# Rearranging the two ends of an attention stage, and filling TensorE's last attention slots with unread products

## The chip, the cores and the metric

The kernel runs on one core of a Trainium2 chip. It is one program, launched once, and the metric is the device time of that launch in microseconds (us). Three runs of the kernel before took 1500.4, 1500.2 and 1497.41 us; their median is 1500.2. The engines are TensorE (PE in the profile, with its weight loads as PEld), VectorE (DVE), ScalarE (ACT), GpSimd (POOL), and SyncE (SP), which here issues every DMA.

## The reference

The reference is one layer of a streaming encoder for two groups of rows: 1024 prompt rows without a cache, and 64 decode rows with a cache of 256 keys. Cut to what matters here:

```
z = (rms_norm(x) * (1 + sc1) + sh1) @ w_in            # queries, keys, values, index queries
lam = exp(sum(lq1*lk1)) - exp(sum(lq2*lk2)) + 0.2
# 4 differential heads:
a = softmax(q1 k1 + bias) - lam * softmax(q2 k2 + bias)
o = rms_norm(a @ v) * g_subln * 0.8
# 8 sparse heads (2 key/value heads): keep the top-k keys of an indexer's score, then
o = softmax(q k + bias, kept keys only) @ v
m = concat(o_diff, o_sparse) @ w_out                  # 1024 x 1024
x = x + ga1 * rms_norm(m)
x = x + ga2 * rms_norm(swiglu(rms_norm(x) * (1 + sc2) + sh2))
```

Keys are visible by chunks of 64 positions, and the bias comes from a table of 32 buckets over key position minus query position. The new keys and values are outputs too.

## The kernel before, in words

Products that need float32 accuracy are made from two parts of each operand: a high part (the value rounded to TensorE's fp32r) and a low part (value minus high part). A product is then three matmuls: high by high, high by low, low by high.

The program has four stages, in the order of time: the input projection with its modulation and the top-k search (0 to about 372 us of the span), attention (372 to 670), the output projection (670 to 780), and the feed-forward network (to the end).

The input projection works through 21 blocks of 128 output columns (`BLOCKS`), each in three chunks of token columns (`chunk`). The last seven blocks but a few are query blocks. ACT copies each query block to `qst`, and SP stores it to `q_scratch` in HBM. Before the last block (`b == NB - 1`) SP loads heads 0 to 6 of the queries of token tile 0 into `qt`; head 7 of tile 0 and the whole of tile 1 are loaded after that block. ACT computes the two exponentials of lambda after the last block (line 1395), and DVE finishes lambda (line 1891).

Attention is a software pipeline written out by hand. There are nine token tiles `t` (eight of 128 prompt rows, one of 64 decode rows) and eight steps per tile (steps 0 to 3 are the differential heads, 4 to 7 the sparse ones, two heads a step), so `NSTEPS` = 72 steps. Each engine runs a loop over `SLOTS` = 78 slots. In a slot it works on different steps: PE makes the scores of step `s` = slot (`scores`), transposes the probabilities of step slot-3 (`transpose_probs`), makes the value products of step slot-4 (`value_products`), and transposes the normalised head of slot-6. DVE adds biases and finds row maxima of step `s` = slot (`biases`, line 1977), and scales the probabilities of slot-2 (`weights`, lines 1914 to 1991). ACT takes exponentials of slot-1 (line 1500) and copies transposed tiles out (`aT`, `oT`). Slots 72 to 77 have no new scores: they drain the pipeline. The order within each engine is the order of the code, and engines wait for each other by semaphores.

The biases come from HBM in expanded form. Tiles 0, 1 and 8 have theirs loaded in one go (`e_first`, `e_second`, `e_last`); tiles 2 to 7 use a ring of four (`ering`, `load_e`, line 909), two DMAs for each of 12 heads of a tile. The name `ering` stands in the trace for `e_second` too (line 927). SP issues all DMAs in the order of its code. After the ring's load number 8 of tile 2 it issues, in one go, the six loads of the decode rows' values (`load_decode_values`, lines 935 to 940), which are first read at slot 68.

While attention drains, the operands of the output projection are prepared. ACT rounds the weight rows to their high part (`oweh`, `split_out`, by the table `W_HIGH`), in the order `W_ORDER` = (4, 5, 6, 7, 3, 0, 1, 2), and the attention output of tile 0 (`oTh_first`, `high_out`). The low parts `owel` of weight blocks 4, 5, 6, 7 are subtracted on POOL in slots 68 to 71 (line 1180), those of 3, 0, 1, 2 on DVE in slots 73 and 74 (line 2042). DVE makes the low part of tile 0's attention output (`low_out(0)`, line 1907) in slot 72. `out_products` (line 2759) then makes, for each tile and each half of the columns, 8 blocks times 3 products; the first tile's first product waits for `o_lo` and the first `owel`. Tile 0 accumulates in the PSUM region called `S` in the trace, tile 1 in `PJ`.

## Time and profile before

| what | value |
|---|---|
| median of three runs | 1500.2 us |
| profiled execution, its time | 1499.62 us |
| its span (first to last instruction) | 1497.9 us |
| PE busy | 1421.3 us (95%) |
| DVE busy | 1065.1 us (71%) |
| ACT busy | 645.0 us (43%) |
| POOL busy | 323.0 us (22%) |
| mean granted TensorE clock | 0.974 |

The shares of busy time are averages over stages with different limits. The granted clock is 1.00 at TensorE's full speed of 2.4 GHz and 0.50 at 1.2 GHz. A row that ends in "[2.33 <-DVE ...]" says that the engine was idle for 2.33 us just before it, and what ended that.

### The profile page before, as it was taken

To read this page: it belongs to the slowest core of one execution; us is meant where nothing else is said; L and a number is where in the kernel's file an instruction comes from. 1 tells how busy PE (TensorE), PEld (TensorE's weight loads), DVE (VectorE), ACT (ScalarE), POOL (GpSimd) and SP (SyncE) were. 2 spreads that over 40 slices of the span, in tenths; PEclk is the share of its full clock that TensorE was granted. 3 is DMA by queue.
4 is the path that set the end of the run, shared out by engine and by line. 5 is a ranking of instruction groups with operands and counts; after the bars stand their busy time and mean duration, and the time that the engine had idled before them with its cause. 6 is when DMAs were issued, how large, how long until landed. Compare 5 with 4: busy or idle time off the path is not lost.

```text
span 1497.9 us, 26711 instructions
## 1 busy us (share of the span) xinstructions
PE 1421.3 (95%) x9519; PEld 1230.4 (82%) x9519; DVE 1065.1 (71%) x2317; ACT 645.0 (43%) x1362; POOL 323.0 (22%) x357
## 2 busy tenths in 40 slices
PE   5998999999789999989997999999999999999997
PEld 3775999899456666658887999999999999888876
DVE  4526999998789888783578666666566656875687
ACT  4546222222577776772564332233223332533353
POOL 3111111111111000030112543344334440000011
PEclk9999999999699999979999999999999999999999
DMA  9410456633555455532323323332333216995333
GB/s 298 126 50 17 133 178 202 204 111 99 113 157 153 145 137 136 117 113 78 115 83 100 97 89 114 86 104 80 114 114 111 73 58 227 307 322 190 115 89 141
DMA packets 180148, 198.28 MB, mean 132 GB/s; under 512 B 19757, under 2 KB 136814, under 8 KB 180058
## 3 DMA queue, kind: packets, MB, share of 16 engines
q1 hardware_dynamic: 180058, 197.11, 43.6%
q8 instruction: 52, 0.85, 0.2%
q14 instruction: 38, 0.31, 0.1%
HBM read 154.00 MB, written 43.08 MB: 132 GB/s over the span
## 4 chain that ended last, share of the span: by engine, by line
PE 86%; DVE 5%; ACT 3%; issue 2%; DMA 2%; SPq 1%; POOL 0%; DVEq 0%; POOLq 0%; ACTq 0%
PE PJ L2506 15%; PE S L2788 14%; PE S L2865 8%; PE T L2788 8%; PE PJ L2788 8%; PE S L2651 5%; PE PJ L2865 4%; PE T L2865 4%; PE S L2759 4%; PE T L2626 3%; PE PJ L2759 3%; PE PJ L2713 2%; PE PJ L2716 2%; PE S L2562 1%; PE S L2657 1%
## 5 line engine op out<-in xcount | busy, mean ns | idle before, releaser
L1794 DVE TENSOR_SCALAR_CACHE_REDUCE scrap<-work,cand 128x384 uint8<-128x384 f32 (+6 forms) x217 | 177.9, 884 | 1.1
L2506 PE MATMUL PJ<-hTh,wh 128*128 128x352 f32 (+2 forms) x480 | 160.7, 335 | 0.0
L2506 PE MATMUL PJ<-hTh,wl 128*128 128x352 f32 (+2 forms) x480 | 157.5, 328 | 0.0
L2506 PE MATMUL PJ<-hTl,wh 128*128 128x352 f32 (+2 forms) x480 | 157.4, 328 | 0.0
L662 POOL TENSOR_TENSOR wab_a<-graw,wab_a 128x512 fp32r<-128x512 f32 x63 | 87.4, 1401 | 247.0 <-ACT wab_a L1396 247.0
L1136 POOL TENSOR_TENSOR wl<-wraw,wh 128x1024 fp32r<-128x1024 f32 (+1 forms) x21 | 49.5, 2358 | 273.8 <-ACT wh L1230 273.8
L2098 DVE TENSOR_TENSOR mix_later<-mix_later,S 128x256 f32<-128x256 f32 (+1 forms) x147 | 60.9, 427 | 66.2 <-PE S L2788 65.2
L2788 PE MATMUL S<-tokA,wab_a 128*128 128x256 f32 x792 | 99.9, 285 | 0.2 <-ACT mix_later L1396 0.2
L2788 PEld LDWEIGHTS S<-tokA,wab_a 128*128 128x128 f32 x792 | 97.9, 193 | 0.6 <-issue 0.5
L2506 PEld LDWEIGHTS PJ<-hTh,wh 128*128 128x128 f32 (+1 forms) x480 | 90.6, 189 | 7.8 <-issue 6.4
L1396 ACT ACTIVATE aT<-T 128x512 f32<-128x512 f32 (+4 forms) x168 | 67.9, 452 | 56.2 <-PE T L2626 55.7
L2506 PEld LDWEIGHTS PJ<-hTl,wh 128*128 128x128 f32 (+1 forms) x480 | 90.8, 189 | 0.3
L2506 PEld LDWEIGHTS PJ<-hTh,wl 128*128 128x128 f32 (+1 forms) x480 | 90.4, 188 | 0.3
L2098 DVE TENSOR_TENSOR hid<-mix_later 128x256 f32<-128x256 f32 (+1 forms) x84 | 71.6, 852 | 25.8 <-ACT mix_later L1554 20.8
L1396 ACT ACTIVATE dhi<-draw 128x1088 fp32r<-128x1088 f32 (+2 forms) x77 | 64.1, 836 | 60.0 <-PE PJ L2865 22.7
L1977 DVE CUSTOM_DVE_ANT_0 sc<-S,ering 128x256 f32<-128x256 f32 (+6 forms) x84 | 65.9, 821 | 24.0 <-PE S L2651 12.9
L1500 ACT ACTIVATE sc<-sc,nmax 128x128 f32<-128x128 f32 (+8 forms) x108 | 79.7, 742 | 0.8 <-DVE nmax L1977 0.8
L1127 POOL TENSOR_SCALAR mss<-mss 128x1 f32<-128x1 f32 (+1 forms) x23 | 5.4, 237 | 303.1 <-ACT ysq L1681 197.0
L2865 PE MATMUL S<-dhi 128*128 128x512 f32 x176 | 68.6, 390 | 0.0
L2865 PE MATMUL S<-dlo,dhi 128*128 128x512 f32 x176 | 68.5, 389 | 0.0
L1549 ACT ACTIVATE mix_later<-mix_later 128x256 f32<-128x256 f32 (+1 forms) x42 | 18.1, 431 | 109.3 <-DVE mix_later L2098 109.3
L1554 ACT ACTIVATE mix_later<-mix_later 128x256 f32<-128x256 f32 (+1 forms) x42 | 17.8, 423 | 106.3 <-DVE mix_later L2098 106.3
(360 smaller groups left out, 3581.6 us busy)
## 6 DMA issues: line engine op xcount, KB each, us to landing
graw<-in_w_gu SPq DMA_DIRECT2D x44, 512.0 KB, 5.4
ada<-in_w_ada SPq DMA_DIRECT2D x16, 1024.0 KB, 7.3
draw<-in_w_down SPq DMA_DIRECT2D x55, 256.0 KB, 3.6
h_scratch<-hid SPq DMA_DIRECT2D x22, 544.0 KB, 3.5
s_scratch<-hsum SPq DMA_DIRECT2D x11, 1024.0 KB, 4.2
draw<-s_scratch SPq DMA_DIRECT2D x44, 256.0 KB, 3.7
wraw<-in_w_in SPq DMA_DIRECT2D x20, 512.0 KB, 5.8
draw<-h_scratch SPq DMA_DIRECT2D x33, 256.0 KB, 3.0
```

What stands on the lines that cost most here:

```text
L662: eng.tensor_tensor(weight_operand(q, 1), weight_source(s, q), weight_operand(q, 0).bitcast(F32), ALU.subtract).then_inc(g_lo, 1)
L1136: pool.tensor_tensor(wl[:, b % 2, :, 0:n], wraw[:, b % 2, :, 0:n], wh[:, b % 2, :, 0:n].bitcast(F32), ALU.subtract).then_inc(w_lo, 1)
L1396: act_copy = lambda out, in_, **kw: nc.scalar.activation(out, in_, ACT.Copy, **kw)
L1500: nc.scalar.activation(p, p, ACT.Exp, scale=-1.0, bias=nmax[0:r, s % 4, m:m + 1], accum_out=rsum[0:r, s % 4, m:m + 1]).then_inc(exp_done, 1)
L1794: ins = nc.vector.tensor_scalar(scrap[0:r, o:o + n], work[0:r, o:o + n], least_score, None, ALU.is_ge, ALU.add, accum_out=rows_at(count, i))
L1977: nc.vector.tensor_tensor_reduce(out=probs(s, m)[0:r, 0:n], in0=S[m][0:r, 0:n], in1=rev, scale=-1.0, scalar=3.0e38, op0=ALU.add, op1=ALU.m ...
L2098: nc.vector.tensor_tensor(to, a, b, op).then_inc(mixed, 1)
L2506: last = pe.matmul(chunk_bank(3 * b + c)[0:w, 0:n], wp[:, b % 2, k, 0:w], hp[:, k, c0:c0 + n], start=(k == 0 and p == 0), stop=(k == KB - ...
L2651: last = pe.matmul(S[m][0:r, o:o + w], qt[part, t % 2, i, 0:r], keys, start=True, stop=not kept)
L2759: last = pe.matmul(OUT[t % 2][0:r, cols_], op[:, k, 0:r], wp[:, k, cols_], start=(k == W_ORDER[0] and p == 0), stop=(k == W_ORDER[-1] and ...
L2788: last = pe.matmul(bank, weight_operand(q, wp)[:, k, :], token_operand(c, q, tp)[:, k, :], start=(k == 0 and p == 0), stop=(k == 3 and p = ...
L2865: last = pe.matmul(down_bank(s, j), ap, wp[:, 0:HD], start=(k == 0 and p == 0), stop=(k == HALF - 1 and p == len(parts) - 1))
```

## The change

Six things change. All are in or beside attention.

1. Heads 0 to 6 of the queries of tile 1 are loaded before the last projection block too (448 KB), right behind those of tile 0; head 7 of tile 1 (64 KB) follows behind head 7 of tile 0. The load of the whole tile 1 (512 KB), which stood behind the loads of `e_second`, is gone. PE waits for head 7 of tile 1 at step 15.
2. ACT makes lambda's exponentials, with the table load they need, between the first and the second chunk of the last projection block.
3. The six loads of the decode values are no longer issued together at tile 2, but one at a time behind ring loads 1, 2, 3, 7, 8 and 9 of tile 5.
4. POOL makes no low part of the output weights any more. All eight are made on DVE, four in slot 73 and four in slot 74.
5. `low_out(0)` moves on DVE from slot 72 to slot 73, and the first half of tile 0's output products is ordered by part: eight high by high products, then eight with the low part of the attention output, then eight with the low part of the weights, each with its own waits.
6. PE gets `IDLE_PRODUCTS` = 4 products at the end of each of slots 72 to 76, 20 in all: `identb` by `upto`, bf16 constants, 128x128 by 128x512, into a PSUM bank that nothing reads before it is overwritten. They wait for the last biases, since the bank held scores.

```diff
-W_LOW_POOL = {68: 4, 69: 5, 70: 6, 71: 7}
-W_LOW_DVE = {73: (3, 0), 74: (1, 2)}
+W_LOW = {73: (4, 5, 6, 7), 74: (3, 0, 1, 2)}
...
+IDLE_PRODUCTS = 4
...
                     load_q(0, 0, 7)
+                    load_q(1, 0, 7)
...
-                if t:
+                if t >= 2:
                     load_q(t, 0, 8)
...
             load_q(0, 7, 8)
+            sp.wait_ge(ld_q[1], 16)
+            load_q(1, 7, 8)
             load_tile(0)
...
-                if j == 8 and t == 2:
-                    load_decode_values()
+                if t == 5 and j in (1, 2, 3, 7, 8, 9):
+                    load_decode_values((1, 2, 3, 7, 8, 9).index(j))
...
-                if slot in W_LOW_POOL:
-                    k = W_LOW_POOL[slot]
-                    pool.wait_ge(ow_hi, W_ORDER.index(k) + 1)
-                    pool.tensor_tensor(owel[:, k, :], owraw[:, k, :], oweh[:, k, :].bitcast(F32), ALU.subtract
-                                       ).then_inc(ow_lo_p, 1)
...
+                    if b == NB - 1 and c == 0:
+                        act.wait_ge(lam_ready, 1)
+                        nc.scalar.activation(lam[:, 2:4], lam[:, 0:2], ACT.Exp).then_inc(lam_ready, 1)
...
-                if slot == NSTEPS:
+                if slot == NSTEPS + 1:
                     low_out(0)
-                for k in W_LOW_DVE.get(slot, ()):
+                for k in W_LOW.get(slot, ()):
...
                 if i == 0:
-                    pe.wait_ge(ld_q[t % 2], 16 * (t // 2 + 1))
+                    pe.wait_ge(ld_q[t % 2], 16 * (t // 2 + 1 + (t % 2 if t > 1 else 0)))
+                if t == 1 and i == 7:
+                    pe.wait_ge(ld_q[1], 32)
...
+                if NSTEPS <= slot < SLOTS - 1:
+
+                    pe.wait_ge(biased, 2 * NSTEPS)
+                    for _ in range(IDLE_PRODUCTS):
+                        pe.matmul(S[1][:, 512:1024], identb[:, :], upto[:, 0:512], start=True, stop=True)
...
+                first = t == 0 and half == 0
+                order = [(p, k) for p in (0, 2, 1) for k in ks] if first else [(p, k) for k in ks for p in range(3)]
```

On SP, between the projection's last blocks and attention, the order before is this (`qt` is filled with queries, `vsbp` with values, `ering` at line 927 is `e_second`):

```order
L886 DMA q_scratch<-qst 128x1088 [waits chunk_out] x2
L864 DMA qt<-q_scratch 128x7x128 [waits q_stored1,q_stored0,score_acc]
L886 DMA q_scratch<-qst 128x1088 [waits chunk_out]
L864 DMA qt<-q_scratch 128x128 [waits r_stored,score_acc,q_stored1,ada_used,nat_stored1,chunk_done,q_stored0,nat_stored0]
L920 DMA vsbp<-out_dv_p 128x512
L921 DMA vsbp<-out_sv_p 128x128
L927 DMA ering<-r_scratch 64x12x192
L927 DMA ering<-r_scratch 64x12x256
L864 DMA qt<-q_scratch 128x8x128
```

The same place on SP in the changed kernel:

```order
L887 DMA q_scratch<-qst 128x1088 [waits chunk_out] x2
L864 DMA qt<-q_scratch 128x7x128 [waits q_stored1,q_stored0,score_acc]
L864 DMA qt<-q_scratch 128x7x128
L887 DMA q_scratch<-qst 128x1088 [waits chunk_out]
L864 DMA qt<-q_scratch 128x128 [waits r_stored,score_acc,q_stored1,ada_used,nat_stored1,chunk_done,q_stored0,nat_stored0]
L864 DMA qt<-q_scratch 128x128 [waits ld_q1]
L921 DMA vsbp<-out_dv_p 128x512
L922 DMA vsbp<-out_sv_p 128x128
L930 DMA ering<-r_scratch 64x12x192
L930 DMA ering<-r_scratch 64x12x256
```

The big load of tile 1's queries has moved from behind `e_second` to a place ahead of the last query store, and one 64 KB load stands newly ahead of the values and of `e_second`.

On DVE at the end of attention (slots 72 to 74 and the first work behind them), before:

```order
L1914 RECIPROCAL rinv<-rsum 64x2 [waits exp_done]
L1988 TENSOR_SCALAR sc<-sc,rinv 64x320 [waits vchain]
L1988 TENSOR_SCALAR sc<-sc,rinv 64x320
L2016 TENSOR_SCALAR ob<-ob,oss 64x128 [waits o_rms]
L1907 TENSOR_TENSOR oTl_116<-oT_94,oTh_first 128x1024 [waits o_hi]
L1914 RECIPROCAL rinv<-rsum 64x2 [waits exp_done]
L1988 TENSOR_SCALAR sc_last<-sc_last,rinv 64x320 [waits vchain]
L1988 TENSOR_SCALAR sc_last<-sc_last,rinv 64x320
L2042 TENSOR_TENSOR owel<-owraw,oweh 128x1024 [waits ow_hi] x4
L1907 TENSOR_TENSOR oTl_117<-oT_95,oTh 128x1024 [waits o_hi]
```

The same place on DVE in the changed kernel:

```order
L1914 RECIPROCAL rinv<-rsum 64x2 [waits exp_done]
L1988 TENSOR_SCALAR sc<-sc,rinv 64x320 [waits vchain]
L1988 TENSOR_SCALAR sc<-sc,rinv 64x320
L2016 TENSOR_SCALAR ob<-ob,oss 64x128 [waits o_rms]
L1914 RECIPROCAL rinv<-rsum 64x2 [waits exp_done]
L1988 TENSOR_SCALAR sc_last<-sc_last,rinv 64x320 [waits vchain]
L1988 TENSOR_SCALAR sc_last<-sc_last,rinv 64x320
L1907 TENSOR_TENSOR oTl_116<-oT_94,oTh_first 128x1024 [waits o_hi]
L2042 TENSOR_TENSOR owel<-owraw,oweh 128x1024 [waits ow_hi] x8
L1907 TENSOR_TENSOR oTl_117<-oT_95,oTh 128x1024 [waits o_hi]
```

The low part of tile 0's output now stands behind the last probabilities, and eight weight subtractions follow it instead of four.

On PE from the last value products (slots 74 and 75) to the first output products, before:

```order
L2713 MATMUL PJ<-aT_92,vsbd 64x64 [waits pair_read,t_freed1,t_freed0]
L2713 MATMUL PJ<-aT_92,vsbd 64x64 x5
L2713 MATMUL PJ<-aT_112,vsbd 64x64 [waits pair_read,t_freed0,t_freed1]
L2713 MATMUL PJ<-aT_112,vsbd 64x64 x5
L2759 MATMUL S<-oweh,oTh_first 128x512 [waits ow_lo_p,o_lo]
L2759 MATMUL S<-owel,oTh_first 128x512
L2759 MATMUL S<-oweh,oTl_116 128x512
L2759 MATMUL S<-oweh,oTh_first 128x512 [waits ow_lo_p]
```

The same place on PE in the changed kernel:

```order
L2715 MATMUL PJ<-aT_92,vsbd 64x64 [waits pair_read,t_freed1,t_freed0]
L2715 MATMUL PJ<-aT_92,vsbd 64x64 x5
L2752 MATMUL S<-upto,identb 128x512 [waits biased]
L2752 MATMUL S<-upto,identb 128x512 x3
L2715 MATMUL PJ<-aT_112,vsbd 64x64 [waits pair_read,t_freed0,t_freed1]
L2715 MATMUL PJ<-aT_112,vsbd 64x64 x5
L2752 MATMUL S<-upto,identb 128x512 [waits biased]
L2752 MATMUL S<-upto,identb 128x512 x3
L2752 MATMUL S<-upto,identb 128x512 [waits biased]
L2752 MATMUL S<-upto,identb 128x512 x3
L2775 MATMUL S<-oweh,oTh_first 128x512 [waits ow_hi,o_hi] x8
L2775 MATMUL S<-oweh,oTl_116 128x512 [waits o_lo] x8
```

Eight unread products stand between the last value product and the first output product, and the output products no longer ask for a low part of the weights before their seventeenth.

## Rows read from the trace of the kernel before

**Rows 1.** Busy time by stretch: attention's start.

```profile
372.00:403.00 31.00, 23.75 (x104) 13.77 (x104) 18.64 (x104) 18.53 (x73) 5.61 (x12) 0.56 0.63 142
```

Columns of such a row: stretch and its length in us; busy us (and count) of PE, PEld, DVE, ACT, POOL; granted clock; DMA share; GB/s.

**Rows 2.** Timeline at attention's start, of ACT, POOL and DVE (start, duration).

```profile
372.63 1.28 ACT L1395 ACT_TABLE_LOAD   x1
...
372.15 0.73 POOL L1155 MEMSET e_first<- 64x768 f32 x1 [19.82 <-PE PJ L2506]
...
374.38 0.29 DVE L1977 CUSTOM_DVE_ANT_0 sc<-S,e_first 128x128 f32<-128x128 f32 x1
```

**Rows 3.** Loads of `e_second`: timeline of SP, and size with us to landing.

```profile
376.83 1.29 SPq L927 DMA_DIRECT2D ering<-r_scratch  x2
...
ering<-r_scratch SPq DMA_DIRECT2D x1, 768.0 KB, 10.4
```

**Rows 4.** Timeline of PE: the scores of steps 8 and 9.

```profile
389.45 1.23 PE L2651 MATMUL S<-kTp,qt 64*128 64x256 f32 x4 [3.36 <-DMA qt<-q_scratch]
...
392.25 1.23 PE L2651 MATMUL S<-kTp,qt 64*128 64x256 f32 x4
```

**Rows 5.** The decode values' loads: SP and DVE, and a stretch behind.

```profile
423.17 0.59 SPq L935 DMA_DIRECT2D vsbd<-in_c_dv  x1
...
430.27 0.56 DVE L1977 CUSTOM_DVE_ANT_0 sc<-S,ering 128x384 f32<-128x384 f32 x1 [2.98 <-DMA ering<-r_scratch]
...
430.30:437.00 6.70, 6.11 (x25) 4.42 (x27) 6.25 (x23) 1.66 (x4) 1.15 (x2) 0.50 0.45 121
```

**Rows 6.** The ring's loads in tile 5: timeline of SP, issue to landing.

```profile
503.38 34.73 SPq L909 DMA_DIRECT2D ering<-r_scratch  x24
...
DMA to landing us min/median/max: 3.0/3.4/4.4
```

**Rows 7.** Attention's end, POOL and DVE: timeline, and one group of lines by form.

```profile
662.04 2.34 POOL L1180 TENSOR_TENSOR owel<-owraw,oweh 128x1024 fp32r<-128x1024 f32 x1
...
648.56 2.30 DVE L1916 SCALAR_TENSOR_TENSOR rlam<-rinv,lam,rsum 64x1 f32<-64x1 f32 x1
...
661.28 3.28 DVE L1988 TENSOR_SCALAR sc<-sc,rinv 64x320 f32<-64x320 f32 x2
...
L1988 DVE TENSOR_SCALAR sc<-sc,rinv 64x320 f32<-64x320 f32 x6 | 8.8, 1502 | 0.1
...
666.00 0.68 DVE L1988 TENSOR_SCALAR sc_last<-sc_last,rinv 64x320 f32<-64x320 f32 x2
666.59 4.61 DVE L2042 TENSOR_TENSOR owel<-owraw,oweh 128x1024 fp32r<-128x1024 f32 x4
```

**Rows 8.** Timeline of ACT in slots 69 to 72.

```profile
650.15 1.06 ACT L1396 ACTIVATE oweh<-owraw 128x1024 fp32r<-128x1024 f32 x1
...
658.77 0.55 ACT L1500 ACTIVATE sc<-sc,nmax 64x320 f32<-64x320 f32 x1
...
659.87 1.04 ACT L1396 ACTIVATE oTh_first<-oT 128x1024 fp32r<-128x1024 f32 x1
660.82 0.65 ACT L1396 ACTIVATE aT<-T 128x128 f32<-128x128 f32 x4
```

**Rows 9.** Stretches around idle times of PE, in attention and in the next stage.

```profile
649.50:651.50 2.00, 0.21 (x3) 0.01 (x1) 1.97 (x3) 1.71 (x5) 1.35 (x1) 1.00 0.10 39
652.50:670.00 17.50, 13.00 (x87) 8.01 (x86) 17.29 (x33) 13.06 (x41) 8.93 (x8) 0.50 0.01 2
...
801.50:804.00 2.50, 0.14 (x2) 0.14 (x2) 2.50 (x5) 2.03 (x4) 0.00 (x0) 1.00 0.00 0
804.00:808.00 4.00, 4.00 (x32) 4.00 (x32) 3.97 (x6) 0.00 (x0) 2.88 (x1) 1.00 0.00 0
```

**Rows 10.** PE: bf16 products of the same size, and timeline at attention's end.

```profile
L2657 PE MATMUL S<-keep,identn 128*128 128x512 bf16 x16 | 4.1, 382 | 0.0
...
669.40 1.10 PE L2713 MATMUL PJ<-aT,vsbd 128*64 128x64 f32 x12 [0.80 <-ACT aT L1396]
...
684.03 0.39 PE L2759 MATMUL PJ<-oweh,oTh 128*128 128x512 f32 x1
```

More of the change, by code:

```diff
@@ L864, in load_q @@
                 sp.dma_start(qt[:, t % 2, i0:i1, 0:r], q_dram[i0:i1, :, 128 * t:128 * t + r]
-                             .rearrange("b p t -> p b t")).then_inc(ld_q[t % 2] if i0 == 0 else ld_q7, 16)
+                             .rearrange("b p t -> p b t")).then_inc(ld_q7 if t == 0 and i0 else ld_q[t % 2], 16)
             for b in range(NB):
@@ L1392, in _ @@
                     row_out(j)
-            act.wait_ge(lam_ready, 1)
-            nc.scalar.activation(lam[:, 2:4], lam[:, 0:2], ACT.Exp).then_inc(lam_ready, 1)
             act_copy = lambda out, in_, **kw: nc.scalar.activation(out, in_, ACT.Copy, **kw)
```

51 lines of the change are left out of this document (29 added, 22 removed).

## The prediction, made before the changed kernel was run

> **What bounds the kernel now.** I read the split by stretch first, with the granted clock, then the list of who waited for whom inside attention, then the timeline of each engine at three places, then the sizes and landing times of DMAs there. PE is busy 95% of the span, so a change that leaves PE's own work alone can only win where PE stands or runs at its low clock. Attention holds three such places. At its start the granted clock is 0.56 on average and PE is busy 23.75 of 31 us [rows 1]. There PE stands 3.36 us for the queries of tile 1 [rows 4]. At 427 us DVE stands 2.98 us for a ring load that SP issued behind the six loads of the decode values, and the clock is 0.50 for the 6.7 us after it [rows 5]. From 652.5 to 670 us the clock is again 0.50, PE is busy 13.00 of 17.5 us and DVE 17.29 [rows 9]: DVE is the bound there, with work that takes much longer than it should [rows 7]. Outside these places I let everything move as one block, because between them the waits go from engine to engine and no transfer has a fixed date.
>
> **The start.** Lambda first. Before, DVE's first bias runs at 374.38, behind ACT's table load of 1.28 us that ends at 373.91 [rows 2]. With the exponentials inside the last block nothing holds that bias but PE's scores and the corner that POOL clears, ready at 372.15 + 0.73 = 372.9 [rows 2]. So slots 0 to 7 can begin up to 1.5 us sooner. That does not pass to the end, since slot 8 meets another limit, below. ACT's table load is hidden by its idle time between chunks; if it were not, it would cost its 1.28 us once.
>
> The queries: the scores of step 8 no longer wait. What is late next is `e_second`, the biases of step 8. Its second DMA is issued at about 376.83 + 0.65 = 377.5 and lands 10.4 us later, at 387.9 [rows 3]. One 64 KB load, some 0.4 us of SP, now stands ahead of it: 388.3. The 448 KB load is long over by then. From there the two bias operations of step 8, of 256 columns, take less than twice the 0.56 us of the 384-column form [rows 5]; I take 0.85. The scores of step 9 then start at about 389.15, where they started at 392.25 [rows 4]. They gain 3.1 us, because the transposes and value products of slot 8 (2.80 - 1.23 = 1.6 us of PE) now lie inside the wait for `e_second` instead of behind it. Bounds: if `e_second` lands 1 us later because other loads have moved ahead, 2.1; if it lands 1 us sooner with no 512 KB behind it, 4.1. From slot 9 on PE is busy without a gap before and after.
>
> The Trainium skill, "DMA: Bandwidth & Descriptors", section "Queues, rings and completion order", says that completion does not follow the order of issue on one engine. By that, `e_second` shared its time with the 512 KB issued behind it, which was down by 389.4 [rows 4], only 1.5 us after it. By the order of issue the landing stays at 388.3; by sharing it would come earlier, near the 4.1 end. No run here shows which yet.
>
> **The decode values.** The DVE wait of 2.98 us [rows 5] goes: the six loads took SP from 423.17 on, each about 0.6 us with the gap to the next, 3.2 us together, so the ring load behind them lands some 3.2 us earlier and is just in time. PE does not stand there, so the low clock of 430.3 to 437 goes too. It was worth little: DVE was busy 6.25 of those 6.70 us [rows 5], so at most 0.45 us was lost; I take 0.5 with the start of the next slot. Sum 3.5 us, between 3.0 and 4.0. In tile 5 each of the six loads adds 0.6 us to SP between ring loads. There 24 ring DMAs, two for each load, are spread over 34.73 us and land in 3.4 us [rows 6], so one ring load comes every 2.9 us and holds SP for 1.2 of it. The ring is four loads deep, 11.6 us on the average; I count nothing.
>
> **The end.** POOL's four subtractions cost 2.34 us each and lie on DVE's work. The clearest pair: POOL works from 662.04 to 664.38, and DVE's two scalings take 3.28 us from 661.28; the same two, with POOL idle, take 0.68 [rows 7]. Six of them took 8.8 us instead of 6 x 0.34 = 2.0, and a 64x1 operation took 2.30 us for what I take as 0.2. That is 8.9 us of stretched DVE time that goes. Against it DVE gets four more subtractions at 4.61 / 4 = 1.15 us [rows 7].
>
> With DVE free the next bound is ACT. Its chain from the end of the third `oweh` copy, 650.15 + 0.95 = 651.1 (such copies follow each other in 0.95 us, 659.87 to 660.82 [rows 8]), to the last transposed probabilities: six copies of 128x1024 (5.7 us), three pairs of exponentials at 1.10 (658.77 to 659.87; 3.3), three and a half groups of four transpose copies at 0.65 (2.25), and six small copies at 0.2 (1.2). Sum 12.45, so it reaches 663.55, and step 71's copies end at 664.2. The last value products start at 664.3, where they started at 669.40 [rows 10].
>
> Then the unread products. The first twelve lie in waits that PE has anyway. The last eight stand on the path: eight times 0.227 us at full clock. That price is from the output products (512 columns at 2.4 GHz are 0.213 us, and their rows at full clock step by 0.227), of which 48 follow each other from 669.40 + 1.10 = 670.5 to 684.03 [rows 10], part of them at the low clock; at 0.227 each 48 take 10.9 us, so 2.6 us were lost to the clock. The bf16 products of the same size in the trace keep PE 4.1 / 16 = 0.26 us each [rows 10], the other bound. So value products 0.6, eight unread 1.8: the output products start at 666.7. DVE's last low part comes at: exponentials of step 71 done at 658.7, scalings to 659.6, then nine subtractions at 1.15, 669.95. The seventeenth product, the first that reads a low weight, starts at 666.7 + 16 x 0.227 = 670.3, so none waits. At full clock the 48 end at 677.6 against 684.03: 6.4 us, less 0.4 for hand-overs that a chain without gaps leaves out, 6.0.
>
> Sum: 3.1 + 3.5 + 6.0 = 12.6 us, from the profiled execution's 1499.6 to 1487.0. The median of the runs is 0.6 above that execution, so 1487.6; I say 1487.5.
>
> **The rivals.** A, the forecast: the clock stays high through the drain. For it: PE's idle times shrink to about 1.4 us each, and unread products lie between. Chance 0.40.
>
> B: the clock falls there all the same. In the trace it fell after PE had stood 1.8 of 2.0 us, and it stayed at 1.00 after PE had stood 2.36 of 2.5 us [rows 9]. So an idle time alone does not decide. My replay leaves two idle times, about 659.7 to 661.2 and 662.6 to 664.3, with 1.5 us of work between, so it is open. Price: value products 1.1, eight unread ones at 0.427 = 3.4, start 668.8; the clock comes back 6.8 us after 664.3 as it did after 669.40 (670.5 + 2.6 / 0.2 = 13 products at 0.427, to 676), so five output products at the low clock and 43 at 0.227: 680.9, 3.3 us worse. Time 1490.8, chance 0.33.
>
> The Trainium skill, "TensorE: Matmul & The Clock Gate", Part 1, says that the point where the clock changes differs from run to run of one kernel. By it A and B would both occur among the runs, and the median would lie anywhere between 1487.5 and 1490.8. It is why I hold neither far above the other.
>
> C: the clock also stays high at the start, since PE's first wait, for the biases that began at 374.38 [rows 2], ends some 1.4 us sooner. Slots 8 to 12 ran at 0.50 with PE as the bound, 2.80 us a slot [rows 4]; at full clock four of them save about 0.7 us each. Time 1484.7, chance 0.12.
>
> D: the start's gain goes to `e_second` or another late transfer and only 0 to 1 us is left of 3.1. Against it: 10.4 us of landing already includes the traffic of that time. Time 1490.1, chance 0.10.
>
> E, slower: each decode load now makes its own stall. Before, six together cost 2.98 us and a fall of the clock. If in tile 5 each of them held the next ring load past its date, six waits would come. The price passes the whole gain of 12.6 us when each wait exceeds 2.1 us; at 3 us each, 18 less 12.6 gives 1505. It decides only if the ring's slack is used up. A load has to be issued and down in the time in which the two or three ahead of it are used, at least 2 x 2.9 = 5.8 us; it needs 1.2 + 0.6 + 3.4 = 5.2. That is closer than the average, but the wait would be tenths, not microseconds. Chance 0.03. The last 0.02 are for no change, if the stretched DVE work came from something else and the ends cancelled.
>
> **How the numbers follow.** A's own range is 1485.5 to 1489.5, from the bounds of the start (1 us either way), the middle (0.5) and the price of the unread products. With B, C and D taken in, 8 in 10 lie in 1483 to 1492.5. Faster by more than 0.2% (3 us), about what a measurement of this kernel can tell from no change, needs less than 1497.2: A to D, 0.95. Within: 0.02. Slower: 0.03.
>
> **What would show it.** In the changed profile: no wait of PE for `qt` at step 8 but one of DVE for `ering` near 388; no gap near 427 and none in tile 5; the scalings of steps 68 to 70 at 0.68 us a pair; ACT without gaps from slot 69 to 74; the output products of tile 0 taking 10.9 us, not 13.5. It is wrong if the pairs stay long with POOL idle, if products seventeen on wait for `owel`, or if the stages behind attention do not simply start earlier.

## The result: 10 us faster, and three attention segments that each tell their share

The changed kernel took 1490.19 us (median of five runs, 1488.58 to 1492.15), the kernel before 1500.2 in the runs beside them (1497.41 to 1502.34). The ratio is 0.9938 with a 95% interval of 0.9925 to 0.995, so it is faster by 0.5 to 0.75%. The forecast was 1487.5, with a range of 1483 to 1492.5. A second set of runs of the same kernel gave 1490.98, ratio 0.9935 (0.9918 to 0.9951).

The profiled execution took 1492.15 us, the longest of the five, with a span of 1490.4. I read it against the profile before between five marks on PE: the scores of step 0, of step 9 and of step 68, the first output product of tile 0, and the first of tile 1. Each column of the table below is the time in us from one mark to the next. Where nothing between two marks differs, such times often agree to tenths of a microsecond, while the totals of single runs differ by 3 to 5 us. The table holds every kernel of the study; the labels are explained with the experiments.

| kernel | scores 0 at | to scores 9 | to scores 68 | to output tile 0 | to output tile 1 | to the last product |
|---|---|---|---|---|---|---|
| before | 372.12 | 20.13 | 251.93 | 26.25 | 13.60 | 805.77 |
| changed | 376.80 | 15.48 | 245.31 | 26.43 | 11.09 | 807.25 |
| before_again | 373.83 | 19.05 | 252.05 | 26.26 | 13.64 | 805.76 |
| after_again | 375.40 | 15.08 | 247.60 | 26.34 | 11.12 | 806.63 |
| lambda_back | 375.00 | 14.77 | 249.14 | 26.46 | 11.11 | 807.01 |
| queries_back | 373.41 | 18.16 | 248.36 | 26.51 | 11.11 | 806.62 |
| decode_back | 373.45 | 15.08 | 251.82 | 25.90 | 11.11 | 806.60 |
| pool_low | 374.04 | 15.03 | 248.34 | 30.50 | 11.09 | 805.58 |
| no_unread | 374.33 | 15.07 | 247.79 | 21.45 | 13.10 | 805.59 |
| by_block | 374.16 | 15.14 | 247.50 | 21.47 | 12.94 | 805.59 |
| unread_early | 373.98 | 14.95 | 248.74 | 21.60 | 12.83 | 806.68 |
| search_gated | 374.68 | 16.75 | 245.45 | 21.48 | 13.38 | 806.65 |
| act_relieved | 373.18 | 17.06 | 248.01 | 18.05 | 13.39 | 805.57 |
| relieved_unread | 371.57 | 16.68 | 248.27 | 18.75 | 12.64 | 805.64 |

In the first pair of profiles attention came 4.68 us later, was 13.60 us shorter (311.91 to 298.31), and the stages behind it took 1.48 us more: 7.4 us in all. In the second pair attention went from 311.00 to 300.14, 10.86 us: 3.97 at the start, 4.45 in the middle, 2.44 at the end. Two pairs do not separate what the change gives from what differs from run to run. The experiments do, one edit at a time: 3.1 us at the start, 3.6 in the middle, 2.3 to 2.4 at the end, 9.1 in all.

**The start.** The first row is the stretch of [rows 1] in the changed kernel, the others two later stretches of it (columns as there):

```profile
372.00:403.00 31.00, 24.50 (x139) 15.54 (x137) 25.81 (x136) 18.70 (x78) 6.74 (x16) 0.83 0.59 131
...
380.00:390.00 10.00, 9.46 (x41) 6.25 (x42) 8.99 (x55) 6.15 (x28) 2.35 (x7) 0.51 1.01 205
390.00:400.00 10.00, 8.39 (x56) 4.48 (x57) 7.96 (x38) 8.30 (x34) 0.63 (x2) 0.98 0.60 123
```

The clock is 0.83 on the mean, against 0.56. It is low only from 380.2 to 390.4. PE's timeline where [rows 4] were:

```profile
388.75 1.23 PE L2653 MATMUL S<-kTp,qt 64*128 64x256 f32 x4
...
392.28 0.70 PE L2653 MATMUL S<-kTp,qt 64*128 64x256 f32 x4 [1.07 <-DVE nmax L1977]
```

The 3.36 us for `qt` are gone. What PE waits for now is DVE's step 8, and DVE stood before it:

```profile
391.45 0.42 DVE L1977 CUSTOM_DVE_ANT_0 sc<-S,ering 128x256 f32<-128x256 f32 x1 [1.65 <-issue]
```

SP's timeline has the two loads of `e_second`, and the row of DMA issues has the size of the second with its us to landing:

```profile
380.04 1.28 SPq L930 DMA_DIRECT2D ering<-r_scratch  x2
...
ering<-r_scratch SPq DMA_DIRECT2D x1, 768.0 KB, 10.7
```

It was issued at 380.04 + 0.63 = 380.7 and landed at 391.3. The profile names no releaser for DVE's 1.65 us, but they end 0.1 us behind this landing. That is the load that the prediction named as next late.

**The drain.** PE's timeline from slot 72 on, to be read against [rows 10]; L2752 are the unread products:

```profile
650.58 0.34 PE L2741 MATMUL T<-ident,ob 64*128 64x64 f32 x1 [1.30 <-ACT aT L1396]
650.85 1.89 PE L2752 MATMUL S<-upto,identb 128*128 128x512 bf16 x4
652.67 0.90 PE L2626 MATMUL T<-ident,sc 64*128 64x64 f32 x6
653.50 1.10 PE L2715 MATMUL PJ<-aT,vsbd 128*64 128x64 f32 x12
...
654.93 1.89 PE L2752 MATMUL S<-upto,identb 128*128 128x512 bf16 x4
...
658.62 1.89 PE L2752 MATMUL S<-upto,identb 128*128 128x512 bf16 x4
660.44 1.11 PE L2715 MATMUL PJ<-aT,vsbd 128*64 128x64 f32 x12
661.48 2.89 PE L2752 MATMUL S<-upto,identb 128*128 128x512 bf16 x8
664.02 2.19 PE L2775 MATMUL S<-oweh,oTh_first 128*128 128x512 f32 x8
```

From 650.58 on no row has an idle time: PE is the bound, and it works at half speed. Four unread products step by 1.82 us (650.85 to 652.67), twice the price that the prediction took. The clock by stretch:

```profile
646.00:650.00 4.00, 2.71 (x28) 1.70 (x25) 3.06 (x14) 3.84 (x13) 1.45 (x4) 0.98 0.02 4
650.00:656.00 6.00, 5.36 (x27) 2.69 (x28) 3.90 (x8) 5.71 (x20) 0.00 (x0) 0.50 0.01 3
656.00:660.00 4.00, 4.00 (x24) 1.90 (x22) 4.00 (x5) 2.16 (x7) 0.00 (x0) 0.50 0.00 0
660.00:664.00 4.00, 4.00 (x22) 1.75 (x21) 4.00 (x5) 1.23 (x2) 0.00 (x0) 0.56 0.32 83
```

It fell at 649.9, before the first unread product, and was back at 663.5. DVE has what the prediction said, where [rows 7] had 3.28 us for a pair:

```profile
649.45 0.67 DVE L1988 TENSOR_SCALAR sc<-sc,rinv 64x320 f32<-64x320 f32 x2
...
654.31 9.15 DVE L2042 TENSOR_TENSOR owel<-owraw,oweh 128x1024 fp32r<-128x1024 f32 x8
```

### The profile page after: what moved, and what is told of

Its sections match the earlier page's. It is cut to its first block, busy times and chain, and to the rows that moved or that the text cites. A ratio compares the mean times of both kernels' runs of the same rounds, so it can differ in the third digit from the quotient of the medians.

```text
span 1490.4 us, 26760 instructions
## 1 busy us (share of the span) xinstructions
PE 1421.1 (95%) x9539; PEld 1228.7 (82%) x9539; DVE 1067.2 (72%) x2321; ACT 644.5 (43%) x1362; POOL 313.8 (21%) x353
## 4 chain that ended last, share of the span: by engine, by line
PE 71%; DVE 21%; ACT 3%; issue 3%; DMA 1%; SPq 0%; POOL 0%; DVEq 0%; POOLq 0%; ACTq 0%
PE S L2805 15%; DVE scrap L1794 13%; PE PJ L2805 8%; PE T L2805 7%; PE S L2882 7%; PE S L2653 5%; PE T L2882 4%; PE S L2775 4%; PE PJ L2506 3%; PE PJ L2882 3%; PE T L2626 3%; PE PJ L2775 3%; PE PJ L2715 2%; PE PJ L2718 2%; PE S L2562 1%
```

## The experiments

Three groups shared their runs of the kernel before: no_unread, pool_low, queries_back and decode_back; after_again, before_again, unread_early and search_gated; lambda_back, by_block and act_relieved. relieved_unread has its own. Each ratio is to the runs of before in its own group.

### no_unread: the changed kernel without the unread products

```diff
-IDLE_PRODUCTS = 4
+IDLE_PRODUCTS = 0
```

> The changed kernel without the 20 unread products; nothing else differs. In its profile the clock had fallen to 0.50 at 649.9, before the first unread product (650.85); twelve of them stood on PE's path at 1.82 us per four, and PE was busy without a gap from 650.58. Theory 1 (they are a cost): ACT's chain becomes the bound (aT of step 71 ready near 657.9), the output products of tile 0 start 4.5 to 5 us earlier (near 659 against 664.02), they run some 11 to 14 of 48 at the low clock (0.427 instead of 0.227 us each, 2.2 to 2.8 us), and tile 1's first product comes 2 to 2.8 us earlier than 675.1. Total 1.5 to 3 us less than the changed kernel. Theory 2 (they bring the clock back, which is worth what they cost): without them PE has gaps until 659 and the low clock lasts into the output products for 30 of 48 or more; total 0 to 2 us more than the changed kernel.

Measured: 1487.1 us, ratio to before 0.9931 (0.9915 to 0.9946). PE in its drain:

```profile
650.17 0.34 PE L2741 MATMUL T<-ident,ob 64*128 64x64 f32 x1 [1.29 <-ACT aT L1396]
...
654.25 0.33 PE L2741 MATMUL T<-ident,ob 64*128 64x64 f32 x1 [1.66 <-ACT aT L1396]
...
657.61 1.10 PE L2715 MATMUL PJ<-aT,vsbd 128*64 128x64 f32 x12 [0.95 <-ACT oT L1396]
658.64 3.78 PE L2775 MATMUL S<-oweh,oTh_first 128*128 128x512 f32 x8
662.22 2.43 PE L2775 MATMUL S<-oweh,oTl 128*128 128x512 f32 x8
```

The waits are ACT's again, the output products start at 658.64, and the first eight take 3.58 us at the low clock:

```profile
660.00:664.00 4.00, 4.00 (x12) 3.10 (x11) 4.00 (x4) 0.00 (x0) 0.00 (x0) 0.61 0.94 359
```

From scores 68 to output tile 1 it takes 34.55 us instead of 37.46 to 37.52. Theory 1 holds, 0.1 us beyond the 2 to 2.8 us that it gave: the unread products cost 2.9 us net. The clock fell at 649.5 here and came back at 663.1, and with them at 649.9 and 663.5. It was low for 13.65 us in both, and back 25.9 us behind scores 68 in both, so they did not bring it back sooner: they put the output products off by 5.0 us (26.43 against 21.45), into a time of full clock, where these take 2.0 us less (11.09 against 13.10). The medians differ by 3 to 4 us, but against their own runs of before the two kernels differ by only 0.6 to 1 us (0.9931 against 0.9938 and 0.9935), with intervals that overlap. So the claim rests on the traces.

### pool_low: four low parts back on POOL

```diff
-W_LOW = {73: (4, 5, 6, 7), 74: (3, 0, 1, 2)}
+W_LOW_POOL = {68: 4, 69: 5, 70: 6, 71: 7}
+W_LOW = {73: (3, 0), 74: (1, 2)}
```

> The changed kernel, with the low parts of weight blocks 4, 5, 6, 7 back on POOL in slots 68 to 71 (order by part and unread products stay). Theory 1 (POOL's subtraction stretches DVE's operations while it runs): the pairs of scalings of steps 68 to 70 take about 2.9 us again instead of 0.67, DVE is the bound of the drain, from the scores of step 68 to the value products of step 71 it takes 25 us or more instead of 22.9, and the total is 2 to 4 us above the changed kernel. Theory 2 (the stretch had another cause, such as the low clock or the traffic of the loads): the pairs stay at 0.67 and the total is within 0.5 us of the changed kernel.

Measured: 1494.78 us, ratio 0.9972 (0.9961 to 0.9982). DVE and POOL in slot 70:

```profile
650.87 2.75 DVE L1995 TENSOR_SCALAR sc<-sc,rinv 64x320 f32<-64x320 f32 x2
```

```profile
650.81 2.34 POOL L1186 TENSOR_TENSOR owel<-owraw,oweh 128x1024 fp32r<-128x1024 f32 x1
```

The three pairs take 2.77, 2.75 and 3.28 us, each beside a POOL subtraction, and a 64x1 operation takes 2.31. From scores 68 to output tile 1 it is 41.59 us, 4.1 more than the changed kernel. Theory 1 holds; its 2 to 4 us were a little low. It is also 1.7 us more than before (39.85): with the stretch in place and the unread products added, the drain is longer than it was.

### queries_back: tile 1's queries loaded behind `e_second`

```diff
-                    load_q(1, 0, 7)
...
-                if t >= 2:
+                if t:
                     load_q(t, 0, 8)
...
-            sp.wait_ge(ld_q[1], 16)
-            load_q(1, 7, 8)
```

> The changed kernel, with tile 1's queries loaded behind the second bias load again. PE stands 3 us or more at step 8. Theory 1 (as I predicted, only the wait itself): 3 us more than the changed kernel, and the slots behind it run at the same clock as with the queries early. Theory 2 (the wait also keeps the clock low until about slot 12): the clock comes back near 400 instead of 390, slots 9 to 12 take 2.4 to 2.8 us instead of 1.6, and the total is 5 to 7 us above the changed kernel. Theory 3 (the early return of the clock was chance): the clock comes back near 390 to 394 all the same, 2 to 3 us more.

Measured: 1494.04 us, ratio 0.9968 (0.9956 to 0.9979). PE at step 8:

```profile
388.77 1.23 PE L2648 MATMUL S<-kTp,qt 64*128 64x256 f32 x4 [3.18 <-DMA qt<-q_scratch]
```

The wait is back. Scores 0 to 9 take 18.16 us instead of the 15.08 of after_again: 3.1 us. From scores 9 to 68 it is 248.36, between the 247.5 and 249.1 of its neighbours. The clock came back 11.6 us behind scores 9 (at 403.2), against 10.5 to 11.2 in after_again, decode_back, pool_low and no_unread. So theory 1 holds, and theory 2 (that the wait keeps the clock low) falls.

### decode_back: the six loads together at tile 2

```diff
-                if t == 5 and j in (1, 2, 3, 7, 8, 9):
-                    load_decode_values((1, 2, 3, 7, 8, 9).index(j))
+                if j == 8 and t == 2:
+                    for n in range(6):
+                        load_decode_values(n)
```

> The changed kernel, with the six loads of the decode values issued together at tile 2, load 8. Theory 1 (SP's queue): DVE stands about 3 us for the ring's load behind them (where the profile before had it at 427), PE's clock falls there, and the total is 3 to 4 us above the changed kernel. Theory 2: with attention's start earlier the ring is not ahead any more or less than before, and the wait is hidden by PE: 0 to 1 us.

Measured: 1493.22 us, ratio 0.9966 (0.9954 to 0.9979). DVE:

```profile
426.59 0.56 DVE L1978 CUSTOM_DVE_ANT_0 sc<-S,ering 128x384 f32<-128x384 f32 x1 [3.13 <-DMA ering<-r_scratch]
```

The wait of [rows 5] is back, and scores 9 to 68 take 251.82 us. The nine variants with spread loads whose clock behaved alike there have 247.50 to 249.14, mean 248.2. The difference is 3.6 us, and theory 1 holds. A rest of the wait is left near 425 us in six of the eleven profiles with spread loads, 0.2 to 0.65 us; the two with the longest (lambda_back and unread_early) have the two longest middles.

By ratio the totals of pool_low, queries_back and decode_back lie 4.2 to 5.5 us above the changed kernel, 0.6 to 1.9 us more than their times between marks. Their intervals are wide enough for both.

### after_again and before_again: each kernel once more

No edit. They ask which differences of the first pair of profiles belong to the change.

> The changed kernel once more. In its first profile the clock at attention's start fell at 380.6 and was back at 390.6, and from the scores of step 9 to those of step 68 it took 245.3 us; the three variants that keep the loads of the decode values spread took 247.8 to 248.4 there, with the low clock from about 377 to 401. Theory 1 (the early return was chance): this time 247.5 to 248.5 us, clock low until 398 to 403, and the attention from the first scores to the first product of the second output tile takes 300.5 to 301.5 us instead of 298.3. Theory 2 (it belongs to this kernel): 245 to 246 us again.

> The kernel before once more, for its profile. In its first profile three of DVE's small operations in the top-k search ran into a POOL subtraction (4.8 us in excess of 0.17 us each) and the search ended at 369.5, ahead of PE; in all five profiles of changed kernels there were five such (8.6 to 10.9 us), the search ended at 373.0 to 376.4 and PE waited 1.6 to 1.8 us. Theory 1 (it differs from run to run): five collisions and a search that ends at 372 or later can come here too, with a first score some 1.5 to 2 us later than 372.1. Theory 2 (the change causes it): three collisions and 369.5 again. From the first scores on both expect 311 to 312.5 us to the first product of output tile 1.

Measured, after_again: 1490.98 us, ratio 0.9935 (0.9918 to 0.9951); scores 9 to 68 in 247.60 us and 300.14 in all. The clock stayed low until 401:

```profile
390.00:400.00 10.00, 10.00 (x42) 4.90 (x41) 5.78 (x27) 6.92 (x28) 0.00 (x0) 0.50 0.33 86
```

Theory 1 holds: the early return in the first profile differs from run to run, and is worth 2 to 3 us. Of the eleven other profiles of changed kernels search_gated had it too; in act_relieved the clock came back at 388.3 and was low again from 391.7 to 401.9.

Measured, before_again: 1500.37 us in its one run. PE waits for the top-k search before the first scores, as in every changed kernel without the gate:

```profile
373.62 0.28 PE L2614 MATMUL T<-ident,gates 128*32 128x128 f32 x1 [1.77 <-DVE lam L1886]
```

Five small operations of the search ran into POOL's subtractions (0.78 + 1.71 + 2.38 + 2.28 + 2.35 = 9.5 us for what takes 0.85), and the search ended at 373.6 instead of 369.6. Theory 1 holds: a late search needs no change of the kernel, though how often the kernel before has one, two profiles can't say. The profile of before on which the prediction rests was one in which the search ended early.

### lambda_back: the exponentials behind the last projection block

```diff
-                    if b == NB - 1 and c == 0:
-                        act.wait_ge(lam_ready, 1)
-                        nc.scalar.activation(lam[:, 2:4], lam[:, 0:2], ACT.Exp).then_inc(lam_ready, 1)
...
+            act.wait_ge(lam_ready, 1)
+            nc.scalar.activation(lam[:, 2:4], lam[:, 0:2], ACT.Exp).then_inc(lam_ready, 1)
```

> The changed kernel with lambda's exponentials behind the last projection block again. Theory 1 (as I predicted: what lambda gives is taken back at step 8, where the bias load is late next): the first bias is 1.5 us or more later behind the first scores (2.2 instead of 0.62), but from the first scores to those of step 9 it takes at most 0.5 us more than 15.1. Theory 2 (the profiles of the variants show no wait for that load; PE at its low clock is the bound of slots 4 to 8, so lambda's 1.6 to 2.0 us are kept): 16.7 to 17.1 us from the first scores to those of step 9, and the attention from the first scores to tile 1's first output product 1.6 to 2.0 us longer than 300.1.

Measured: 1491.54 us, ratio 0.9938 (0.9917 to 0.996). Neither theory: the first bias stands 0.62 us behind the first scores (375.62 and 375.00), as with the edit, and scores 9 come after 14.77 us. PE and DVE wait for the search here, and ACT's table load is over by then. before_again, without the edit, has 0.62 us there too (374.45 and 373.83). In this state of the search the lambda edit gives nothing. In the first profile of before, with the search early, it would have given up to the 1.64 us by which that first bias was later (2.26 against 0.62).

### by_block: output products ordered by weight block again, on no_unread

```diff
-order = [(p, k) for p in (0, 2, 1) for k in ks] if first ...
+order = [(p, k) for k in ks for p in ((0, 2, 1) if first else range(3))] if first ...
```

> The kernel without unread products, with the first half of tile 0's output products ordered by weight block again (for each block high by high, low by high, high by low). Theory 1 (the order by part is what lets them start before the low weights are there): DVE has finished the first low part about 3 us before they start and needs 1.15 us for each further one, three products at the low clock need 1.28 us and at full clock 0.68; from the time the clock is back they would catch up with DVE near the sixth block and wait 0 to 1 us in all. Theory 2 (the order does nothing once DVE starts early): from the last value products to tile 1's first product 14.1 us as in the kernel without unread products, within 0.3. Both expect a small number; a wait for owel in the trace decides.

Measured: one run, 1486.6 us. PE has no wait for `owel`, and from the scores of step 68 to output tile 1 it takes 34.41 us against 34.55. Theory 2: with DVE free early, the order by part gives nothing that one profile could tell.

### unread_early: the unread products in slots 70 to 73

```diff
-                if NSTEPS <= slot < SLOTS - 1:
-                    pe.wait_ge(biased, 2 * NSTEPS)
+                if 70 <= slot < 74:
+                    pe.wait_ge(biased, 2 * min(slot + 1, NSTEPS) - 2)
```

> The changed kernel with the unread products in slots 70 to 73, four each, instead of 72 to 76. They now begin at about 647, while the clock is still high (it fell at 649.3 to 649.9). Theory 1 (PE's idle times make the clock fall, and products in them prevent it): the clock stays at 1.00 through the drain; the value products of step 71 come at ACT's pace, about 20.4 us behind the scores of step 68 as without unread products, tile 0's 48 output products take 10.9 us, and from the scores of step 68 to tile 1's first product it takes 32 to 33 us (37.5 in the changed kernel, 34.6 without unread products). Theory 2 (the clock falls all the same, since PE has too little dense work for longer than this): 36 to 37.5 us, because eight to twelve of them run at 0.43 to 0.47 us each on the path.

Measured: 1488.48 us, ratio 0.9923 (0.9906 to 0.9939). The clock was still high where it had been low in both other versions:

```profile
650.00:656.00 6.00, 3.53 (x39) 2.05 (x34) 3.99 (x9) 5.89 (x20) 0.02 (x1) 1.00 0.01 3
656.00:660.00 4.00, 3.95 (x34) 2.91 (x33) 4.00 (x4) 2.97 (x9) 0.00 (x0) 0.54 0.00 0
```

It fell at 656.3, in spite of them. The segment takes 34.43 us, as without any. So neither theory's number: products put where the clock is high do hold it for a while, and here the gain and the price were equal.

### search_gated: POOL's subtractions in the projection kept off the search's small operations, on no_unread

```diff
+SEARCH_GATE = {11: 157, 12: 179, 13: 212, 14: 234, 15: 267,
+               16: 289, 17: 311, 18: 344, 19: 355, 20: 377}
...
             for b in range(2, NB):
+                if b in SEARCH_GATE:
+                    pool.wait_ge(vchain, SEARCH_GATE[b])
                 low_w(b)
```

> The kernel without unread products, in which POOL's subtraction of the low part of each projection weight block from 11 to 20 waits until the first count of a chosen round of the top-k search is over, so that it lies beside DVE's long counting operations and not beside the four small ones between rounds. Theory 1 (a small DVE operation stands for as long as POOL's subtraction runs, the long ones do not): no small operation of the search over 0.3 us behind 215 us of the span, the search ends at 363 to 366 instead of 373 to 374, PE does not wait for lambda's copy, the first scores come 1.5 to 1.9 us earlier, at 372 to 372.5; total 1.5 to 2 us below the kernel without unread products if nothing else gives. Theory 2 (the long operations are stretched as well): the search ends within 2 us of 373. Theory 3 (the gates hold the low weights back too long): PE stands for them, and the total is slower by what it stands.

Measured: 1487.32 us, ratio 0.9917 (0.9902 to 0.9932). The pairs behind this experiment, POOL and DVE in the changed kernel:

```profile
282.89 2.38 POOL L1140 TENSOR_TENSOR wl<-wraw,wh 128x1024 fp32r<-128x1024 f32 x1 [13.55 <-ACT wh L1229]
...
282.97 2.33 DVE L1843 TENSOR_SCALAR step<-step 128x7 f32<-128x7 f32 x1
```

A 128x7 operation took 2.33 us because POOL had begun 0.08 us earlier. The same operation by form between 215 and 365 us, in the changed kernel and in the gated one (busy us, mean ns):

```profile
L1843 DVE TENSOR_SCALAR step<-step 128x7 f32<-128x7 f32 x21 | 7.9, 378 | 0.7
```

```profile
L1846 DVE TENSOR_SCALAR step<-step 128x7 f32<-128x7 f32 x22 | 3.8, 170 | 0.7
```

All four kinds of small operation have 166 to 170 ns now, the long counting ones their old times, and the search ends at 365.4 instead of 373 to 376. So theory 1 holds for the search. It does not for the total: PE did not wait for the search, yet its first scores came at 374.68, because its own clock had been 0.83 in the stretch from 140 to 160 us, as in the first profile of the changed kernel. The gain against no_unread cannot be told from nothing. Where the first scores did come early, loads took most of it back: in relieved_unread, gated too, they came at 371.57, but scores 9 only 16.68 us later, where the profiles with early queries and without the gate have 14.8 to 15.5. PE stood 1.31 us there for a load of values (`vsbp`) and 0.31 us behind `e_second`.

### act_relieved: ACT's copies of the drain moved, on search_gated

```diff
-W_HIGH = {67: (4,), 68: (5,), 69: (6,), 70: (7,), 72: (3, 0), 73: (1, 2)}
+W_HIGH = {66: (4,), 67: (5,), 68: (6,), 69: (7,), 72: (3,), 73: (0,), 74: (1, 2)}
...
-                if slot == NSTEPS - 1:
+                if slot == NSTEPS - 7:
                     high_out(0)
```

> The kernel without unread products and with the gated search, with ACT's eight copies of the drain moved: the high part of tile 0's output in slot 65 instead of 71, the high parts of weight blocks 4, 5, 6, 7 in slots 66 to 69 instead of 67 to 70, those of 3, 0, 1, 2 in slots 72, 73, 74, 74 instead of 72, 72, 73, 73, the last two behind the last transposed probabilities. Theory 1 (in the drain ACT is the bound once POOL's subtractions are gone): about 2 us leave ACT's chain before the exponentials of step 71 and 2 to 3 us more before its last transposed copies; from the scores of step 68 to the value products of step 71 it takes 16.5 to 18 us instead of 20.4, and to tile 1's first product 31 to 33 us instead of 34.6. Theory 2 (PE at its low clock is as near a bound as ACT): 19.5 us or more to the value products, and 34 us or more to tile 1.

Measured: 1483.26 us (1481.6 to 1485.04), ratio 0.9882 (0.9861 to 0.9902), the lowest of the study. PE at the end of attention:

```profile
654.16 2.22 PE L2718 MATMUL PJ<-aT,vsbd 128*64 128x64 f32 x24
656.30 3.78 PE L2778 MATMUL S<-oweh,oTh_first 128*128 128x512 f32 x8
```

From the scores of step 68 to output tile 0 it takes 18.05 us instead of 21.48, to tile 1 31.44 instead of 34.86. Theory 1 holds: with POOL's subtractions off DVE, ACT's chain was the bound, and 3.4 us could be taken out of the drain by shortening it.

### relieved_unread: the same with unread products in slots 70 to 73

The edits of act_relieved and of unread_early together.

> The fastest kernel so far (no unread products behind slot 74, gated search, ACT's copies moved), with 16 unread products in slots 70 to 73, where the clock is still high. With them in the changed kernel the clock held until 656.3 instead of 649.5, fell in a stretch in which PE was busy 0.72 of 2 us, and the time to tile 1 was the same as without them (34.4 against 34.6 us). Here ACT's chain is 3 us shorter, so PE's idle times are. Theory 1 (the clock then holds to the output products): from the scores of step 68 to the value products of step 71 17 to 18 us, tile 0's 48 products in 10.9 to 11.2 us instead of 13.4, and to tile 1's first product 29 to 30.5 us instead of 31.4. Theory 2 (the clock falls in the drain all the same, or the products cost on PE what the clock gives): 31 to 32.5 us.

Measured: 1484.89 us, ratio 0.9901 (0.9884 to 0.9917). The clock held:

```profile
650.00:656.00 6.00, 5.32 (x59) 3.46 (x57) 4.98 (x7) 5.74 (x19) 0.00 (x0) 1.00 0.00 0
656.00:660.00 4.00, 4.00 (x19) 3.14 (x18) 4.00 (x5) 1.89 (x3) 0.00 (x0) 1.00 0.85 306
```

But the full clock brought PE to another wait:

```profile
655.27 2.18 PE L2778 MATMUL S<-oweh,oTh_first 128*128 128x512 f32 x8
...
660.99 0.50 PE L2778 MATMUL S<-owel,oTh_first 128*128 128x512 f32 x1 [0.34 <-DVE owel L2045]
662.12 0.50 PE L2778 MATMUL S<-owel,oTh_first 128*128 128x512 f32 x1 [0.63 <-DVE owel L2045]
```

Theory 1 is right about the clock and theory 2 about the time: 31.39 us against 31.44. The products took 0.7 us before the output products, and of the 2.3 us that 48 products at full speed would save, 1.5 went into DVE's last low parts (12.64 us against the 11.1 of the changed kernel).

## Why the prediction was right, point by point

**The total** is inside the range, 2.7 us above the value. The likeliest case was not what happened: the clock fell in the drain, which is B, priced at 1490.8. The end gave 3.6 us less than forecast. The total misses by less, because the rest gave more than its terms: the shares found by experiment sum to 9.1 us, the medians to 10.0, and the attention of the second pair to 10.86. Of the 1.8 us between 9.1 and 10.86, 0.9 lie at the start: in before_again tile 1's queries landed 12.1 us behind the start of their issue, in queries_back 11.0. No term of the forecast stood for this, so that part of the nearness is luck.

**The start, 3.1 us.** The size is right: taking the edit back costs 3.1 (18.16 against 15.08). The absolute place, scores 9 at 389.15, was met only in variants (389.4, 389.1 and 388.5 in no_unread, pool_low and decode_back). In the changed kernel's own two profiles scores 9 came at 392.28 and 390.48, in the first no earlier than the 392.25 of before, because the first scores were late. The reason given was half right. PE waits behind `e_second` at step 9 where its slots ran ahead of that load: in the first profile (1.07 us) and in the three gated kernels (0.3 to 1.2). In the others with early queries DVE stands only 0.3 to 0.9 us for it, and PE, at its low clock, is busy 9.6 to 9.8 of the 10 us from 380 on and takes just as long: the wait is gone, and PE's own work is what is left. The Trainium skill's "DMA: Bandwidth & Descriptors", "Queues, rings and completion order", says that completion does not follow the order of issue, from which the prediction took that the landing could come earlier. The traces give that weak support: without the 512 KB behind it the load took 9.4 to 10.7 us in eleven profiles (mean 9.9), with them 10.1 to 11.2 in three (mean 10.6). The ranges overlap.

**Lambda.** It was counted at nothing, and gave nothing, but not because step 8 took it back: DVE's search ended so late that ACT's table load was hidden. Of the eleven profiles without the gate the first profile of before is the only one in which the search ended early.

**The middle, 3.5 us.** Right: 3.6 us by decode_back, 3.8 from the two profiles of before to the mean of the variants. Rival E did not come; no profile with spread loads has a wait for a ring load in tile 5.

**The end, 6.0 us.** Here the sum failed; 2.3 to 2.4 us came. Three steps were right: the stretch of DVE beside POOL (pool_low), ACT's chain as the next bound (act_relieved), and no wait for `owel` in the changed kernel. Two sizes were wrong. "The first twelve lie in waits that PE has anyway" failed: at the low clock they are 5.5 us (3 x 1.82) where PE had 1.66 + 0.95 us of waits left, so that they made PE the bound. And "eight times 0.227 us at full clock" became 2.54 us (661.48 to 664.02), since the clock came back only at 663.5, behind the first five of them. Without the unread products the end gives 5.3 us. That is 0.7 less than forecast: 48 output products take 13.1 us there and not 10.9, but they start 1 us earlier behind scores 68 (21.45 against 22.5, which had 1.8 us of unread products in it). ACT's chain itself was well sized: the last value products stand 20.4 us behind scores 68 in no_unread, with 20.1 forecast.

**B's price.** Forecast for the case of the low clock: 36.7 us from scores 68 to output tile 1 (its own terms give 0.2 less, 680.7 and not 680.9). Measured 37.5. That is near, but by two errors of opposite sign. B charged the low clock only from the last value products on, so that the output products would start 24.6 us behind scores 68; the clock fell at 649.9, the first twelve unread products cost too, and they started at 26.4. And B had the clock low into the output products, 12.1 us for 48 of them; it was back before they began, and they took 11.1.

**C.** A clock that stays high at the start, as C has it, came in no profile. But it was back at 390.4 instead of 401.0 in one of two profiles of the changed kernel. That was worth 2.3 us between them (245.31 and 247.60), near C's 2.8. The Trainium skill, "TensorE: Matmul & The Clock Gate", Part 1, says that the point of change differs from run to run. At the start of attention the traces agree (390.4 and 401.0). In the drain they hardly show it: the fall moves by about 1 us (11.2 to 12.4 us behind scores 68 in the changed kernel's two profiles, lambda_back, queries_back and decode_back), the low stretch is 13.65 us in all five, and the six profiles of kernels with all 20 products behind slot 71 have 11.09 to 11.12 us from the first output product to tile 1. So A, expected in some of the runs by that rule, came in neither profile.

**What was not in the prediction.** First the later start of attention, 4.68 us in the first pair of profiles: PE's projection ended 2.7 us later, after a low clock between 140 and 160 us, and PE then stood 1.78 us for the search. Neither needs the change: before_again has the wait (1.77 us), and seven of the twelve profiles of changed kernels have no low clock there. Then the 1.5 us behind attention. The last column of the table has two groups, 805.6 to 805.8 and 806.6 to 807.3, over kernels with the same code there. In the changed kernel's profile PE stands once for a low part that DVE makes:

```profile
1279.43 0.50 PE L2882 MATMUL S<-dhi 128*128 128x512 f32 x1 [0.97 <-DVE dlo L2313]
```

That wait separates the groups: all seven profiles of the upper one have it (0.4 to 0.97 us), none of the seven of the lower one has. Why DVE is late there in some runs was not tried. The kernel before was twice in the lower group and the changed kernel twice in the upper, but lower ones with the change exist (pool_low, no_unread, by_block), so whether it plays a part is open. Nor was it settled why the clock comes back at 390 in some runs and at 401 in others. The two profiles with the early return are the only two with 6.8 us of low clock near 145 us; three others had 3.4 us there (after_again, lambda_back, act_relieved), and in them the clock was back at 401.0, 398.7 and, in two pieces, 401.9.

## What to carry to other kernels

Work that nobody reads is free only in a wait, and at the clock which it meets: price it at the granted clock of the rows around it, and ask first whether that clock has not fallen before the filler begins. Before an engine is relieved, look who is next, and take work from that one in the same edit: here POOL's subtractions, ACT's copies, the low clock and DVE's low parts lay one behind the other. The drain was 39.9 us, then 34.6 without the first, 31.4 without the second, and still 31.4 without the low clock. And take a second profile of both kernels: in the first pair a later start of 4.7 us and an early return of the clock worth 2 to 3 us, of opposite sign, would have been read as effects of the change.

## What the runs showed of the hardware

- Small DVE operations that started while POOL subtracted two 128x1024 operands in SBUF (in the pair of [rows 7], during POOL's small operation just ahead of that) ended only when POOL was done: a 128x7 operation of 0.17 us took up to 2.42 us (lambda_back), a 64x1 one 2.31 (pool_low) instead of 0.21, and the two 64x320 scalings 2.75 to 3.28 instead of 0.67. The counting operations of the search (0.53 to 1.28 us) kept their times in all profiles.
- In the search this cost 4.8 us in one profile of the kernel before, 8.7 in the other, and 10.8 and 9.7 in the two of the changed kernel, with the same instructions; what differed was where ten POOL subtractions fell.
- In the drain the clock fell at 649.9 with PE busy 2.71 of 4 us before, and it stayed at 1.00 with PE busy 3.53 of 6 us behind unread products (unread_early). Once it had fallen it was low for 13.65 us in the changed kernel, with PE busy without a gap from 650.6, and for 13.65 us in no_unread too, with PE busy 4.14 of 6 and 3.05 of 4 us.
